# A two-layer fp32 denoiser on one core: three half-width block sweeps become part whole, four units share the second stream, and the opening is reordered

## The reference

```python
ada = lambda t, g, shift, scale: rms_norm(t, g) * (1 + scale) + shift
ffn = lambda t, pre: swiglu(t, w_gate, w_up, w_down)          # 1024 -> 2816 -> 1024
x = x + 0.5 * m(2) * ffn(ada(x, lp['norm_ffn1'], m(0), m(1)), 'ffn1')
y, yc = token_mix(ada(x, lp['norm_mix'], m(3), m(4)), ...)    # attention x3, SSM, gates, w_out
x = x + m(5) * y
x = x + 0.5 * m(8) * ffn(ada(x, lp['norm_ffn2'], m(6), m(7)), 'ffn2')
# the same for the context; m(i) = (silu(c) @ w_mod + b_mod) in nine parts; at the end rms_norm
```

## Time and profile before

| | |
|---|---|
| median of 3 runs | 2187.9 us |
| the profiled execution | 2188.3 us, its span 2186.5 us |
| TensorE busy | 2146.8 us (98%) |
| VectorE, ScalarE, GpSimd busy | 1447.5, 1022.0, 616.9 us |
| mean granted TensorE clock | 0.998 of full speed |

### The profile page before, as it was taken

The page is one execution under the profiler, slowest core; times in us unless marked ns, Lnnn a source line. Parts: engine busy times, 40 slices in busy tenths (PEclk is TensorE's granted clock), DMA queues, the critical chain, the costliest instruction groups (busy, mean ns, idle before and its releaser), DMA issues.

```text
span 2186.5 us, 32383 instructions
## 1 busy us (share of the span) xinstructions
PE 2146.8 (98%) x12181; PEld 1793.6 (82%) x12181; DVE 1447.5 (66%) x2042; ACT 1022.0 (47%) x1621; POOL 616.9 (28%) x615
## 2 busy tenths in 40 slices
PE   7999999999999999999999999999999999999998
PEld 4888878987766778987888898888889887889997
DVE  4887887775577456876676784445448858776555
ACT  4544445554455543553344453222235556645444
POOL 0566566402000036344444420000003201261000
PEclk9999999999999999999999999999999999999999
DMA  9476675633343354745545464444546445576564
GB/s 305 149 221 189 171 216 162 177 94 90 97 116 88 90 171 130 207 143 162 155 147 175 128 197 145 145 142 148 153 125 165 116 121 153 152 206 175 184 187 135
DMA packets 471966, 340.64 MB, mean 156 GB/s; under 512 B 13226, under 2 KB 437654, under 8 KB 471686
## 3 DMA queue, kind: packets, MB, share of 16 engines
q1 hardware_dynamic: 441312, 238.06, 37.6%
q0 software_dynamic: 29056, 96.35, 15.1%
q10 hardware_dynamic: 1446, 4.19, 0.5%
HBM read 326.96 MB, written 12.36 MB: 155 GB/s over the span
## 4 chain that ended last, share of the span: by engine, by line
PE 90%; DVE 5%; ACT 2%; issue 2%; DMA 1%; POOL 0%; SPq 0%; DVEq 0%; ACTq 0%; POOLq 0%
PE bank L832 20%; PE bank L833 20%; PE bank L837 19%; PE bank L900 4%; PE bank L910 4%; PE bank L901 3%; PE bank L984 2%; PE bank L990 2%; PE bank L985 2%; DVE w_lo L801 1%; PE bank L1358 1%; PE bank L1334 1%; PE bank L1125 1%; PE bank L1132 1%; PE bank L1126 1%
## 5 line engine op out<-in xcount | busy, mean ns | idle before, releaser
L801 DVE TENSOR_TENSOR w_lo<-raw,w_hi 128x1024 fp32r<-128x1024 f32 (+1 forms) x442 | 583.5, 1322 | 527.3 <-PE bank L837 312.6
L791 ACT ACTIVATE w_hi<-raw 128x1024 fp32r<-128x1024 f32 (+1 forms) x442 | 461.7, 1045 | 621.3 <-PE bank L833 289.2
L832 PE MATMUL bank<-h_hi,w_hi 128*128 128x512 f32 (+1 forms) x1728 | 601.5, 360 | 2.7 <-DVE X L2047 1.5
L833 PE MATMUL bank<-h_lo,w_hi 128*128 128x512 f32 (+1 forms) x1728 | 592.5, 355 | 0.0
L832 PEld LDWEIGHTS bank<-h_hi,w_hi 128*128 128x128 f32 x1728 | 326.5, 189 | 58.9 <-issue 11.8
L837 PE MATMUL bank<-h_hi,w_lo 128*128 128x512 f32 (+1 forms) x1728 | 367.1, 355 | 0.0
L833 PEld LDWEIGHTS bank<-h_lo,w_hi 128*128 128x128 f32 x1728 | 326.7, 189 | 45.4 <-issue 1.0
L837 PEld LDWEIGHTS bank<-h_hi,w_lo 128*128 128x128 f32 x1728 | 291.5, 189 | 45.5
L832 PE MATMUL bank<-inner_hi,w_hi 128*128 128x256 f32 (+1 forms) x654 | 206.2, 337 | 0.0
L833 PE MATMUL bank<-inner_lo,w_hi 128*128 128x256 f32 (+1 forms) x654 | 203.3, 332 | 0.0
L2470 POOL DMA_DIRECT2D wm<-in_w_mod_dram x128 | 92.6, 724 | 362.0 <-DVE gstage L2031 159.3
(11 more groups left out here) (305 smaller groups left out, 3483.3 us busy)
## 6 DMA issues: line engine op xcount, KB each, us to landing
wm<-in_w_mod_dram POOLq DMA_DIRECT2D x128, 512.0 KB, 4.0
raw<-in_w_in_dram SPq DMA_DIRECT2D x108, 512.0 KB, 3.9
raw<-in_ffn_w_down_dram SPq DMA_DIRECT2D x94, 512.0 KB, 3.9
raw<-in_ffn_w_gate_dram SPq DMA_DIRECT2D x88, 512.0 KB, 4.1
raw<-in_ffn_w_up_dram SPq DMA_DIRECT2D x88, 512.0 KB, 4.0
raw<-in_w_out_dram SPq DMA_DIRECT2D x24, 512.0 KB, 4.1
raw<-in_ffn_w_down_dram SPq DMA_DIRECT2D x24, 384.0 KB, 3.9
raw<-in_w_branch_dram SPq DMA_DIRECT2D x16, 512.0 KB, 4.6
```

What stands on the lines that cost most here:

```text
L791: act.activation(w_hi[w_slot[n]][:, 0:unit.rows, :], raw[unit.slot][:, 0:unit.rows, :], ACT.Copy).then_inc(hi_made, 1)
L801: dve.tensor_tensor(w_lo[w_slot[n]][:, 0:unit.rows, :], raw[unit.slot][:, 0:unit.rows, :], w_hi[w_slot[n]][:, 0:unit.rows, :].bitcast(F32) ...
L832: pe.matmul(psum, w_hi[s][:, k, :], hi, start=(k == 0), stop=False)
L833: mm = pe.matmul(psum, w_hi[s][:, k, :], lo, start=False, stop=False)
```

## The change

In the four sweeps of `HALVED` a step is now a block and one or both streams. `w_out` stays as it was (16 steps). The three feed-forward sweeps have 13 steps: blocks 0, 1 and 2 for both streams at once (512 wide), then blocks 3 to 7 for stream 0 and blocks 3 to 7 for stream 1. Each has three units fewer. The norm of stream 0 still begins at step 8, so 5 of its 8 blocks come in the sweep and 3 behind it. The `late` steps end two before the last instead of one. The last inner chunk before these sweeps is no longer made in two halves.

In the quads with both streams the second stream is now done by all four units together, 0, 0, 2 and 2 blocks behind (the first quad of the kernel too). In the opening the second reciprocal stands behind stream 0's norm, a root that has no use is issued early so that its table is loaded there, and `run_on` is gone.

The core of the diff:

```diff
+WHOLE_STEPS = 3
+def whole_steps(l, name):
+    if (l, name) not in HALVED:
+        return DC
+    return 0 if name == "out" else WHOLE_STEPS
+def step_block(l, name, i):
+    return i if i < DC else i - DC + whole_steps(l, name)
+def step_streams(l, name, i):
+    whole = whole_steps(l, name)
+    return range(2) if i < whole else range(i // DC, i // DC + 1)
...
 def ends_in_halves(l, ffn, part, j):
-    return (l, (ffn, part)) in HALVED and j == 2 * PARTS[part][1] - 1
+    return whole_steps(l, (ffn, part)) == 0 and j == 2 * PARTS[part][1] - 1
 def sweep_steps(l, name):
-    return PARTS[name[1]][1] if by_tokens(l, name) else DC * sweep_halves(l, name)
+    return PARTS[name[1]][1] if by_tokens(l, name) else 2 * DC - whole_steps(l, name)
...
                 for st in streams(n):
                     last = st == streams(n)[-1]
-                    if key == (0, 1) and st == 0:
+                    if last and n == TOK or key == (0, 1):
                         pe.wait_ge(lo_made, units[u0].product + 1)
-                        pair_pass(range(u0, u0 + 4), st, last, bank[0:4], (0, 2, 4, 6), key)
+                        pair_pass(range(u0, u0 + 4), st, last, bank[0:4], (0, 0, 2, 2) if last else (0, 2, 4, 6), key)
                         continue
...
                     turn_modulation(MOD_FIRST // 4 - 1)
-                    run_on(8)
...
@@ ScalarE, block_splits @@
-                        square(key, d % DC, d // DC)
+                        square(key, step_block(l, name, d), step_streams(l, name, d) if halved else streams(n)[-1:])
...
+                if halved:
+                    for k in range(sweep_steps(l, name) - DC, DC):
+                        norm_hi(key, k, 0)
@@ ScalarE, opening @@
+            act.activation(early_root[:, 7:8], eps_col[:, 0:1], ACT.Sqrt)
@@ VectorE, add_block @@
-                    late = halved and DC < d < sweep_steps(l, name) - 1
+                    late = halved and DC < d < sweep_steps(l, name) - 2
...
                 if halved:
-                    norm_lo(key, DC - 1, 0)
+                    for k in range(sweep_steps(l, name) - DC, DC + 1):
+                        if k < DC:
+                            norm_scale(key, k, 0)
+                        norm_lo(key, k - 1, 0)
@@ VectorE, opening @@
-                    for st in range(2):
-                        norm_invert((0, 1), st)
+                    norm_invert((0, 1), 0)
                     modulation_vectors(0, "in")
                     for st in range(2):
+                        if st == 1:
+                            norm_invert((0, 1), 1)
@@ GpSimd, add_squares @@
+                for k in range(1, whole):
+                    squares.wait(pool, (key, k, 1))
+                    before = wa[:, 0, :] if k == 1 else wb[:, 1, :]
+                    pooled.done(pool.tensor_tensor(wb[:, 1, :], before, wa[:, k % 2, :], ALU.add), (key, k, 0))
```

More of the change, by code:

```diff
@@ L655, in stream_cols, with step_cols @@
             return slice(st * LAT, (st + 1) * LAT)
+        def step_cols(l, name, i, n):
+            if (l, name) not in HALVED:
+                return slice(0, n)
+            sts = step_streams(l, name, i)
+            return slice(sts[0] * LAT, (sts[-1] + 1) * LAT)
         def next_modulation(l, name, d):
@@ L748, in _ @@
                                  ((0, DC), w_branch[l].rearrange("k (c p) n -> p (k c) n", p=P)[:, :, d * P:(d + 1) * P]))
-                        for again in range(sweep_halves(l, "out")):
-                            stage(first["out", l] + again * DC, DC, lambda j: [((0, DC), columns(w_out, l, j * P))])
+                        for u0, block in sweep_loads(l, "out", first["out", l]):
+                            stage(u0, DC - block, lambda j: [((0, DC), columns(w_out, l, (j + block) * P))])
                     for part, (c0, n) in enumerate(PARTS):
@@ L767, in _ @@
                             continue
-                        for again in range(sweep_halves(l, (ffn, part))):
-                            stage(first["down", l, ffn, part] + again * DC, DC, lambda j: [((0, n), columns(wd, l, j * P, n, c0))])
+                        for u0, block in sweep_loads(l, (ffn, part), first["down", l, ffn, part]):
+                            stage(u0, DC - block, lambda j: [((0, n), columns(wd, l, (j + block) * P, n, c0))])
             for t in range(2):
@@ L1164, in inner_ready @@
                     def inner_ready(k):
-                        if k == rows - 1 and (l, (ffn, part)) in HALVED:
+                        if k == rows - 1 and whole_steps(l, (ffn, part)) == 0:
                             half_lo.wait(pe, (l, ffn, part))
@@ L2045, in add_block @@
                     dve.wait_ge(unit_done, u0 + d + 1)
-                    for st in [d // DC] if halved else streams(n):
-                        ins = dve.scalar_tensor_tensor(out=X[:, d % DC, stream_cols(st)], in0=bank[4 + d % 2][:, stream_cols(st)],
-                                                       scalar=gatev[:, gate_i, d % DC, st:st + 1],
-                                                       in1=X[:, d % DC, stream_cols(st)], op0=ALU.mult, op1=ALU.add)
+                    block = step_block(l, name, d)
+                    for st in step_streams(l, name, d) if halved else streams(n):
+                        ins = dve.scalar_tensor_tensor(out=X[:, block, stream_cols(st)], in0=bank[4 + d % 2][:, stream_cols(st)],
+                                                       scalar=gatev[:, gate_i, block, st:st + 1],
+                                                       in1=X[:, block, stream_cols(st)], op0=ALU.mult, op1=ALU.add)
                     ins.then_inc(added, 1)
```

25 lines of the change are left out of this document (14 added, 11 removed).

## The result

The changed kernel takes 2201.9 us (median of 6 runs, 2199.8 to 2202.4) against 2188.4 for the kernel before in the same comparison: ratio 1.0058, 95% interval 1.0048 to 1.0068. The forecast was 2194.8 with a range up to 2198.5. The direction was right, the size half of what came: +13.5 in place of +6.9. The profiled execution took 2201.86.

The account below looks back on a forecast made before the run. TensorE, busy 98% of the span, was taken as the bound. Terms -2.5 - 2.3 - 0.6 - 0.95 + 6.8 + 2.3 + 4.1 = +6.9 on 2188.3 gave 2195.2, forecast as median 2194.8, range 2189 to 2198.5.

Parts of the forecast that it names:

- its idle time plus 0.16: Pricing rule for TensorE waits: a real stall is 0.16 us more than the idle time shown.
- a rival had a chance of 0.11: Opening: without the eight matmuls the clock falls longer, costing 1.7 us, 2196.5; chance 0.11 together with a seam rival.
- (e): Quads behind three shortened sweeps: norm of three blocks behind the sweep makes TensorE wait, 2.3 us each, +6.8.
- (g): Layer 0's feed-forwards: the chain through the weighted sums makes the seventh unit wait longer, +3.5 and +0.6 us.
- (a): Three sweeps: three blocks each as one 5.44 us step instead of two of 2.86, -2.5 us.
- (b): Start of four quads: first low weight part ready earlier, so TensorE's wait goes, 4 x 0.6, -2.3 us.
- (c): Entry to the sweeps: last inner chunk no longer halved, whole-width matmuls cover TensorE's two waits, -0.6 us.
- (d): Opening: one reciprocal fewer ahead of stream 0's norm, its quad moves earlier, -0.95 us.
- Their own absence is worth 0: Opening: dropping the eight useless matmuls gains nothing, since they end before the first useful one starts.
- (f): Handover behind three feed-forward quads with both streams: the fifth unit waits for the bank silu reads, +2.3 us.
- the slack rival: Behind the first quads the weighted-sum chain has slack, so handover costs partly fail: 4.1 less, 2190.7; chance 0.17.
- the forecast's own tests: Trace signs: whole steps 5.4 us apart, first matmul about 40.2, named waits, TensorE's idle time up some 8 us.

Follow-up runs that it names:

- the sweeps alone: Kernel before with only the change's sweeps (whole steps, earlier end of late splits), first quad and opening as before: 2194.7 us, ratio 1.0028.
- the first quad in pairs: Changed kernel with stream 1 of the kernel's first quad in two pairs of units again: 2196.0 us, ratio 1.0035 to the kernel before.
- filled waits: Changed kernel with useless matmuls put into four long TensorE waits, in three quads and ahead of the seventh unit: 2198.9 us, ratio 1.0046 to the kernel before.
- the late split alone: Kernel before with VectorE's weight split ahead of the norm's work in the last step but one of four halved sweeps: 2187.1 us, ratio 0.9992.
- the opening alone: Kernel before with only the new opening (second reciprocal later, early table load, no useless matmuls): 2188.5 us, ratio 0.9999.
- the order experiment: Changed kernel with VectorE's norm work ahead of the weight's low part in a halved sweep's last step: 2198.9 us, ratio 1.0047 to the kernel before.
- the quads alone: Kernel before with only the second stream of the two-stream quads done by four units together, sweeps and opening as before: 2197.8 us, ratio 1.0039.
- the best kernel: One whole block a sweep, quads in pairs, new opening with eight useless matmuls kept, norm ahead of the last two steps' splits: 2183.9 us, ratio 0.9979.

## Why the prediction was half of what came

**What failed first: the clock.** The forecast priced a wait at its idle time plus 0.16. It asked for the clock only in the opening, where a rival had a chance of 0.11, shared with another, and a price of 1.7 us, and never where terms (e) and (g) made new waits that came as 2.3 and 4.1 us. It had the sign in hand: the earlier trace rows show the clock at 0.50 in the opening, and the trace of before has a fall behind a wait of 2.79 in the last layer too:

```profile
1987.34 0.36 PE L984 MATMUL bank<-h_hi,w_hi 128*128 128x256 f32 x1 [2.79 <-DVE h_lo L1961]
...
1988.00:1992.00 4.00, 4.00 (x23) 3.90 (x22) 3.79 (x8) 1.63 (x4) 0.00 (x0) 0.60 0.78 104
```

What came: behind the wait of 4.10 a low stretch in all three kernels that had it, for 1.6, 2.6 and 1.6 us; behind the waits of 2.27 in four of nine quads, for 1.1 to 1.2 each (the changed kernel two of three, the sweeps alone one, the first quad in pairs one). Filled waits: none of four. In the changed kernel that is 1.63 + 1.17 + 1.22 = 4.0 of the 6.65 missing. That standing still is the cause is shown by the filled waits, where nothing but the filling is changed; why one wait of 2.27 brings it and the next doesn't is open. It is not the same in all executions of one kernel either: the mean granted clock of the changed kernel is 0.995 in four of its six and 0.993 in two.

**(e), forecast 6.8, came 8.3 without the clock** (3 x 2.78). The mechanism was right, place and length (a wait at the third block's end, then 0.35 more). The first wait was 2.43 with its 0.16, not 2.0: ScalarE's w_hi started 0.36 behind the quad's start, behind h_hi of block 3 (434.09), so w_lo began at +1.44 and not at +1.0. The forecast let h_hi end 0.45 too soon, and that is the scaling ahead of it, which took 0.95 beside GpSimd's add and not 0.48.

**(a), forecast 2.5, came 1.1.** The forecast took a whole unit's 5.44 from units whose input is h. The sweep's units, with `inner` as input, go at 0.2325 us a matmul in both traces (mean over more than 1,000), units with h at 0.2275. 24 of them are 5.58, and a block saves 0.12 where 0.28 was counted. The rule of the Trainium skill that the forecast weighed and set aside ("TensorE: Matmul & The Clock Gate", Back-to-back issue gap) gives 0.5 in all, and was nearer to 1.1 than the forecast.

**(b) held:** -0.60, -0.53, -0.56, -0.61, together -2.3; the late split alone shows it too. **(c), -0.6:** the three sweeps together shift -1.99, of which (a) has 1.1, so 0.9 is left for the entry. That is a remainder, no run has (c) alone.

**(d), forecast -0.95, came -0.47.** VectorE did nearly what was forecast (its scaling 0.80 earlier, 37.33 against the earlier trace rows), but ScalarE's h_hi started 0.43 behind that scaling's end where it had been 0.09, and this takes 0.33 back. Its second weight split is not the reason, as the opening alone shows, and the reason is open. And this gain hangs on the clock: of the five kernels without the eight matmuls it was kept in two (the changed kernel, the order experiment) and gone in three (the opening alone, the filled waits, the first quad in pairs). "Their own absence is worth 0" was wrong by up to 0.6.

**(f) and (g), forecast 2.3 and 4.1, came 2.0 and 4.5.** The handovers cost 0.66 each, with 0.51 idle; the seventh unit of layer 0's feed-forwards came 3.6 and 0.8 later, layer 1's 0.1. The chain through the weighted sums has no slack, and the slack rival is out: the quads alone and the first quad in pairs give the same numbers from both sides.

**Together,** measured less forecast: clock +4.0, (e) +1.5, (a) +1.4, (d) +0.5, (g) +0.4, (f) -0.3, (c) -0.3, unchanged code -0.5, in all 6.7 for the 6.65 missing. Without the falls of the clock the time would be some 2197.9, inside the range: the clock is what takes it out.

By the forecast's own tests the waits stood where it said, though the whole steps were 5.59 apart and not 5.4, and the first quad began at 40.73 and not 40.2. The test that failed is the sum: TensorE's idle time (gaps over 0.06 us) grew by 12 us, not 8, of which 2.5 lie in the opening behind VectorE, and 4.0 of the loss is in no idle column at all.

## What to carry to other kernels

A new wait on the bounding engine can be dearer than its length: look whether the clock falls behind it, and give the price of a fall as a part of its range. Work put off behind a phase is free only while the next phase has a lead: here one block's norm cost nothing once it stood ahead of the split, the second 1.2 us, and each was traded for 0.12. Take a pace from instructions with the same operands, not just the same shape.

## What the hardware showed that was not expected

- The half clock came behind waits of 2.27 us in four of nine equal places, and not in the other five; the same place differs from kernel to kernel (layer 0's mixer: 0.50 in two, 1.00 in a third).
- In code that no kernel changed, TensorE waits 1.6 or 1.9 us at one place of layer 1 (1954.88 before). Behind 1.90 (seven traces) the clock fell in three, behind 1.58 (six) in none; in the best kernel:

```profile
1951.12 0.36 PE L890 MATMUL bank<-h_hi,w_hi 128*128 128x256 f32 x1 [1.90 <-issue]
...
1952.00:1955.00 3.00, 3.00 (x16) 3.00 (x16) 2.41 (x6) 1.88 (x4) 0.74 (x1) 0.50 0.20 59
```

In that code and the quad behind it traces differ by up to 2.3 us, mostly by whether the clock is low at these two places (about 1952 and 1990). How much of the spread among executions of one kernel comes from there is not shown.

- Seventy-one useless matmuls in four waits made the kernel faster: 2198.9 against 2201.9.
- Matmuls of 512 columns start 0.2325 us apart in the feed-forward's down product and 0.2275 in units on h, in one and the same trace.
- VectorE's scaling of a block took 0.95 with a GpSimd add beside it, at most 0.49 without.
